# Depthwise convolution of a fused network: who builds the block matrices, who adds the taps, who sums the chunks

## The chip, the cores and the metric

One Trainium2 chip, one of its cores. The metric is the device time of one execution in microseconds, the median of several. The kernel is one program for a whole small network of four layers on 512 tokens with 1024 features.

## The reference, cut to what matters

The first block has two layers. Layer 0 is an attention mixer with an MLP behind it; layer 1 is a convolution mixer with an MLP behind it. The second block (a recurrent and a linear-attention layer) isn't touched. The convolution mixer is

```
a = h @ w_pw1 + b_pw1                                  # 1024 -> 2048
u = a[..., :1024] * sigmoid(a[..., 1024:])
u = causal_depthwise_conv(u, w_dw) + b_dw              # 31 taps, each feature by itself
u = silu(layernorm(u, ln_g, ln_b))                     # over the 1024 features
return u @ w_pw2 + b_pw2
```

The MLP is `square(relu(h @ w1)) @ w2` with 4096 hidden features. All of it is float32 in and out.

## The kernel before, in words

**Products.** A weight matrix streams in "units" of 128x1024 numbers through rings of four slots. For each unit ScalarE rounds the weights (`w_hi`, line 1247), GpSimd subtracts to get the rest (`w_lo`, line 2564), and TensorE multiplies three times (lines 670 to 672: high by high, low by high, high by low). ScalarE may round unit u+3 once TensorE has finished unit u-1, so GpSimd has the time of three units to bring in the rest of a unit before TensorE needs it. Each engine runs its own program in order; they meet at semaphores only.

**The convolution.** Features lie on the partitions, in 8 chunks of 128. For each chunk g the product `pw1{g}` (two units, 16 for the eight chunks) gives the linear part and the gate. VectorE multiplies both by the row of reciprocal norms (`by_row`, line 1841), ScalarE takes the sigmoid (line 1465), and VectorE makes the gated input `conv_u` of the chunk (lines 2113, 2116). Then the 31 taps of a chunk are done in one of three ways:

- Chunks 0, 2 and 7, and taps 0 to 25 of chunk 3, on VectorE: one multiply-and-add over 128x512 for each tap (line 2075), in two running sums that alternate ("lanes", function `tap`). Chunks 0 and 7 are split into two sums that one more add joins (line 2088).
- Chunk 1, and taps 26 to 30 of chunk 3, on two engines: ScalarE multiplies (`tap_product`, line 1448) into one of three `conv_product` buffers, and GpSimd adds (`add_product`, line 2616). Product n therefore waits for the add of product n-3. The last seven products go into the space of chunk 4's block matrices once TensorE has used them (`LATE`).
- Chunks 4, 5 and 6 on TensorE: SyncE's DMAs turn the input into four phases (`conv_phases`), and 9 matmuls a phase with block matrices (`conv_toeplitz`) give the result (line 941, 216 rows in the trace). ScalarE copies it out with the bias (line 1473) and DMAs turn it back into `conv_c` (line 2758). The block matrices of a chunk are built by four instructions (`build_toeplitz`, line 430): chunk 6's on VectorE beside layer 0's MLP (`TOEP_EARLY`), chunk 5's on VectorE right after that MLP and ahead of everything of the convolution, chunk 4's on GpSimd between the splits of the first `pw1` units (`TOEP_POOL`).

Chunk g's taps for ScalarE and GpSimd are handed out at rows k = 1, 3, 5 and 7 of the eight rows of each later `pw1` product, on ScalarE as on GpSimd; what is left is done behind `pw17`.

**The mean.** TensorE then sums the features over the partitions by a product with a matrix of ones into one bank, in this order: chunks 4, 5 (line 949), 1 (951), 6 (953), 3 (955), the sum of chunks 0 and 2 which GpSimd makes in `conv_sum` (957, the sum is line 2640), and 7 (959). Each of these seven is two matmul rows. The bank goes to VectorE, which subtracts it from every chunk (lines 2129, 2126), ScalarE squares (1481), TensorE sums the squares (967), ScalarE takes the root, VectorE the reciprocal, and normalising, silu and `pw2` follow; 34 small transposes (line 764) keep TensorE at work in between. GpSimd adds the bias of `pw2` to the residual (line 2645) as soon as it has made `conv_sum`.

Of the kernel before, what the change touches and what calls it, by code (L numbers as in the profile page):

```python
# [9 lines left out]
ALU = mybir.AluOpType  # L10
# [15 lines left out]
CONV_W = 31  # L26
# [169 lines left out]
CONV_TAPS = list(range(CONV_W))  # L196
# [3 lines left out]
PHASES = 4  # L200
# [1 line left out]
SHIFTS = (CONV_W - 1 + PHASES - 1) // PHASES + 1  # L202
PH_LEN = S // PHASES
PE_GROUPS = [(k, g) for k in PE_CHUNKS for g in range(PHASES)]
TOEP_POOL = [(4, j) for j in range(PHASES)]
TOEP_EARLY = [(6, j) for j in range(PHASES)]
TOEP_DVE = TOEP_EARLY + [(5, j) for j in range(PHASES)]
POOL_TAPS = {1: CONV_TAPS, 3: CONV_TAPS[26:]}
DVE_TAPS = {0: CONV_TAPS, 2: CONV_TAPS, 3: CONV_TAPS[:26], 7: CONV_TAPS}
POOL_ADDS = [(k, i) for k in POOL_TAPS for i in POOL_TAPS[k] if (k, i) != (1, 0)]  # L210

LATE = len(POOL_ADDS) - 7
# [15 lines left out]
def build(nc, a, out):  # L228

    ctx = ExitStack()  # L230
    with ctx:
# [62 lines left out]
        with ExitStack() as scope:  # L294
            cu = sb("conv_u", [P, KD, PAD + S], scope=scope)
            sb("place_of_conv", [P, 16], scope=scope)
            cc = sb("conv_c", [P, KD, S], scope=scope)
# [145 lines left out]
        def signal(name, keys, step=1):  # L443
            return Signal(ctx.enter_context(nc.semaphore(name)), keys, step)
# [21 lines left out]
        def done(name):  # L466
            return used.at(UNITS[name][-1])
# [57 lines left out]
        lag_in = signal("conv_lags_landed", range(PHASES * (len(PE_CHUNKS) + 2)), 16)  # L525


        part_added = signal("conv_made_on_gpsimd", TOEP_POOL + POOL_ADDS + [("sum", 2)])
        dve_tapped = signal("conv_toeplitz_then_taps_made", TOEP_DVE + [0, 2, 3, 7])
        turned_in = [signal(f"conv_turned_landed{n}",  # L530
                            [(w, k, i) for w, k in keys for i in range(PHASES)], 16)
                     for n, keys in enumerate(([("phases", k) for k in PE_CHUNKS] + [("back", 4), ("back", 6)], [("back", 5)]))]
# [127 lines left out]
        def tensor_program(e):  # L660
            w = Waits(e)
# [273 lines left out]
            for k, g in PE_GROUPS:  # L935
                b, n = PHASE_BANKS[g], PE_CHUNKS.index(k)
                empty(b)
                w.wait_ge(*phases_in(k))
                w.wait_ge(*(part_added if k == 4 else dve_tapped).at(k, PHASES - 1))
                for d in range(SHIFTS):  # L940
                    m = e.matmul(bank[b][:, 0:PH_LEN], toep[:, n, g, d, :],  # L941
                                 u4[:, n, g, d:d + PH_LEN], start=d == 0, stop=d == SHIFTS - 1)
                m.then_inc(*mean_mm.up(k, g))
                free[b] = cent_sq.at(k, g)
            empty(MEAN_BANK)
            mean = bank[MEAN_BANK]
            for k in (4, 5):
                w.wait_ge(*back_in(k))
                e.matmul(phase_of(mean[:, :]), mean_ones, phases(cc[:, k, :]), start=k == 4, stop=False)
            w.wait_ge(*part_added.at(1, CONV_W - 1))  # L950
            e.matmul(mean[:, :], mean_ones, cc[:, 1, :], start=False, stop=False)
            w.wait_ge(*back_in(6))
            e.matmul(phase_of(mean[:, :]), mean_ones, phases(cc[:, 6, :]), start=False, stop=False)
            w.wait_ge(*part_added.at(3, CONV_W - 1))
            e.matmul(mean[:, :], mean_ones, cc[:, 3, :], start=False, stop=False)
            w.wait_ge(*part_added.at("sum", 2))
            e.matmul(mean[:, :], mean_ones, csum[:, :], start=False, stop=False)
            w.wait_ge(*dve_tapped.at(7))
            e.matmul(mean[:, :], mean_ones, cc[:, 7, :], start=False, stop=True).then_inc(*mean_mm.up("mean"))

# [273 lines left out]
        def scalar_program(e):  # L1234
# [201 lines left out]
            def tap_product():  # L1436
                k, i = tap_due.pop(0)
                src, weight = cu[:, k, i:i + S], V("dw_w", k * CONV_W + i)
                w.wait_ge(*u_out.at(k))
                if (k, i) == (1, 0):  # L1440
                    e.activation(cc[:, k, :], src, ACT.Identity, scale=weight,
                                 bias=V("dw_b", k)).then_inc(*part_out.up(k, i))
                    return
                if products[0] >= LATE:
                    w.wait_ge(*mean_mm.at(PE_CHUNKS[0], PHASES - 1))
                elif products[0] >= 3:
                    w.wait_ge(part_added.sem, len(TOEP_POOL) + products[0] - 2)
                e.activation(product_at(products[0]), src, ACT.Copy, scale=weight).then_inc(*part_out.up(k, i))
                products[0] += 1

            tap_due, products = [], [0]
            for g in range(KD):
                for k in stream(f"pw1{g}"):
                    if g == 0 and k in (1, 2):
                        for kk in (2 + 2 * k, 3 + 2 * k):
                            round_x(2, kk, HIGH[kk % 4], done("up013"))
                    elif g == 0 and k == 3:
                        take_root(2)
                    elif g == 0 and k == 6:
                        copy_row(1, HIGH[2], rrow)  # L1460
                    elif g and k:
                        if k % 2 and tap_due:
                            tap_product()
                w.wait_ge(*gate_out.at(g))
                e.activation(gate[g % 2][:, :], gate[g % 2][:, :], ACT.Sigmoid,
                             bias=V("pw1_b", KD + g)).then_inc(*gated.up(g))
                tap_due += [(g, i) for i in POOL_TAPS.get(g, [])]
# [345 lines left out]
        def vector_program(e):  # L1813
# [180 lines left out]
            def mlp(layer):  # L1994
                n = 1 + 2 * layer
                for half in range(2):
                    for g in range(4):
                        if half == 0 and g == 0:
                            for k in range(4, KD):
                                split_x(n, k, other(BANKS[f"up{layer}00"])[k % 4])  # L2000
                            take_rstd(n)
                        for j in range(4):
                            w.wait_ge(*f_kept.at(layer, half, 4 * g + j))
                            if g or half:
                                w.wait_ge(*(f_lo.at(layer, half, 4 * g - 4 + j) if g else f_lo.at(layer, 0, 12 + j)))
                            e.tensor_tensor(f_square[j][:, :], f_relu[j][:, :], f_relu[j][:, :],  # L2006
                                            ALU.mult).then_inc(*f_squared.up(layer, half, 4 * g + j))
                        for j in range(4):
                            k = 4 * g + j
                            w.wait_ge(*f_hi.at(layer, half, k))  # L2010
                            e.tensor_tensor(FL[:, k, :], f_square[j][:, :], FH[:, k, :].bitcast(F32),
                                            ALU.subtract).then_inc(*f_lo.up(layer, half, k))
                        if layer == 0 and early:

                            w.wait_ge(*lag_in.last())
                            w.wait_ge(*done("dsa_out1"))
                            chunk, j = early.pop(0)
                            build_toeplitz(e, chunk, j).then_inc(*dve_tapped.up(chunk, j))
                    for m in range(2):
                        name = f"down{layer}{half}{m}"  # L2020
                        if half == 0:
                            add_tiles(BANKS[name], done(name), down_added, layer, m, n=m, scale=n)
                            continue
                        if m == 1:
                            for k in range(4):
                                split_x(n + 1, k, other(BANKS[name])[k])
                        add_tiles(BANKS[name], done(name), updated, n + 1, m, n=m, scale=n)
# [8 lines left out]
            diagonals(1, stat(2, 2))  # L2036
            w.wait_ge(*done("down011"))
            ph_padded = own_dve.after(e.memset(u4[:, :, :, 0:SHIFTS - 1], 0.0))
            for k, j in TOEP_DVE[len(TOEP_EARLY):]:
                build_toeplitz(e, k, j).then_inc(*dve_tapped.up(k, j))  # L2040

            jobs, lanes, lane_mark, turn, side_done = [], [None, None], [None, None], [0], []
# [510 lines left out]
        def gpsimd_program(e):  # L2553
# [63 lines left out]
                                ALU.add).then_inc(*part_added.up(k, i))  # L2617
                added[0] += 1

            due, added, builds = [], [0], list(TOEP_POOL)  # L2620
            for g in range(KD):
                k = 0
                for u in UNITS[f"pw1{g}"]:
                    for kk in range(units[u].per):
                        if g and k % 2 and due:
                            add_product()
                        if kk == 0:
                            split_to(u + AHEAD)
                            if builds and (g or k):
                                w.wait_ge(*lag_in.last())  # L2630
                                w.wait_ge(*done("down011"))
                                chunk, j = builds.pop(0)
                                build_toeplitz(e, chunk, j).then_inc(*part_added.up(chunk, j))
                        k += 1
                due += [(g, i) for i in POOL_TAPS.get(g, [])]
            split_to(UNITS["pw20"][0] + RING)
# [1 line left out]
                add_product()  # L2638
            w.wait_ge(*dve_tapped.at(2))
            e.tensor_tensor(csum[:, :], cc[:, 0, :], cc[:, 2, :], ALU.add).then_inc(*part_added.up("sum", 2))  # L2640

            def add_bias(n):
                w.wait_ge(*row_in.at("b_pw2"))
# [232 lines left out]
```

## Time and profile before

| | |
|---|---|
| median of 3 timed runs | 1791.7 us (1790.89, 1791.70, 1794.44) |
| the profiled execution's own time | 1793.03 us |
| its span (first to last instruction) | 1791.2 us |
| TensorE (PE) busy | 1769.1 us, 99% |
| VectorE (DVE) busy | 822.3 us, 46% |
| GpSimd (POOL) busy | 787.6 us, 44% |
| ScalarE (ACT) busy | 734.5 us, 41% |
| mean granted TensorE clock | 0.997 |

The stage of the convolution is some 140 of these 1791 us: `pw1` on TensorE from about 632 to 720.4 us, the block matrices until 744.5, the mean until 750.9, the norm until 763.3, then `pw2`. The share of an engine over the whole span says little about this stage: there VectorE and GpSimd have few pauses.

### The profile page before, as it was taken

The page shows a single profiled execution, that of the slowest core. Times are in us where ns is not written, and L with a number is a line of the kernel's source. Part 1 is how long each engine was busy: PE and PEld are TensorE (multiplying, and loading weights), DVE is VectorE, ACT ScalarE, POOL GpSimd, SP SyncE. Part 2 cuts the span into 40 slices and gives each one's busy share as a digit, 9 for nine tenths or more (in the row PEclk, how much of TensorE's full clock was granted, in tenths as well). Part 3 has the DMA queues.
Part 4 walks back from the last instruction along what each step waited for, and adds up shares of the span by engine and source line. Part 5 has one row for each costly group of instructions (what it writes and reads, how often), then busy time and mean ns, then how long its engine had stood idle before and what let it go on. Part 6 is the DMA issues. An engine that isn't in the chain of part 4 may idle for free.

```text
span 1791.2 us, 20518 instructions
## 1 busy us (share of the span) xinstructions
PE 1769.1 (99%) x8105; PEld 1452.8 (81%) x8105; DVE 822.3 (46%) x1334; ACT 734.5 (41%) x1152; POOL 787.6 (44%) x351
## 2 busy tenths in 40 slices
PE   9999999999999999999999999999999999998998
PEld 7888778888888878888888888877777888887887
DVE  4794542310121189932210121177877850358643
ACT  5534444321332334554321232355535542455543
POOL 4343224544444469834444444344544544334221
PEclk9999999999999999999999999999999999999999
DMA  6232112333332323223333332333323323232111
GB/s 208 74 108 71 59 48 81 97 106 97 103 95 94 94 82 101 77 71 95 95 94 95 102 97 95 106 107 94 95 86 91 94 94 106 71 110 72 58 60 47
DMA packets 108544, 162.51 MB, mean 91 GB/s; under 512 B 12352, under 2 KB 38592, under 8 KB 108448
## 3 DMA queue, kind: packets, MB, share of 16 engines
q1 hardware_dynamic: 108448, 161.20, 29.6%
q8 instruction: 64, 1.05, 0.2%
q14 instruction: 32, 0.26, 0.0%
HBM read 157.51 MB, written 2.10 MB: 89 GB/s over the span
## 4 chain that ended last, share of the span: by engine, by line
PE 95%; DVE 3%; ACT 1%; issue 0%; DMA 0%; DVEq 0%; SPq 0%; ACTq 0%
PE bank L670 28%; PE bank L672 28%; PE bank L671 28%; PE bank L997 1%; PE bank L941 1%; PE bank L871 1%; PE bank L756 1%; PE bank L853 1%; PE bank L1156 1%; PE bank L1141 1%; DVE rg_u L2178 1%; PE bank L861 0%; DVE rg_u L2175 0%; PE bank L1151 0%; PE bank L1122 0%
## 5 line engine op out<-in xcount | busy, mean ns | idle before, releaser
L2564 POOL TENSOR_TENSOR w_lo<-w_raw,w_hi 128x1024 fp32r<-128x1024 f32 (+1 forms) x286 | 707.1, 2477 | 956.6 <-ACT w_hi L1247 956.6
L1247 ACT ACTIVATE w_hi<-w_raw 128x1024 fp32r<-128x1024 f32 (+1 forms) x286 | 301.0, 1056 | 578.2 <-PE bank L672 572.8
L670 PE MATMUL bank<-x_hi,w_hi 128*128 128x512 f32 (+1 forms) x1264 | 503.6, 398 | 0.3 <-DVE x_lo L2354 0.3
L672 PE MATMUL bank<-x_hi,w_lo 128*128 128x512 f32 (+1 forms) x1264 | 493.0, 390 | 0.0
L671 PE MATMUL bank<-x_lo,w_hi 128*128 128x512 f32 (+1 forms) x1264 | 492.4, 390 | 0.0
L670 PEld LDWEIGHTS bank<-x_hi,w_hi 128*128 128x128 f32 (+1 forms) x1264 | 236.9, 187 | 54.3 <-issue 5.5
L671 PEld LDWEIGHTS bank<-x_lo,w_hi 128*128 128x128 f32 (+1 forms) x1264 | 237.0, 188 | 52.9 <-issue 4.8
L672 PEld LDWEIGHTS bank<-x_hi,w_lo 128*128 128x128 f32 (+1 forms) x1264 | 236.8, 187 | 50.8
L670 PE MATMUL bank<-w_hi,f_hi 128*128 128x512 f32 x512 | 200.2, 391 | 0.0
L672 PE MATMUL bank<-w_hi,f_lo 128*128 128x512 f32 x512 | 199.5, 390 | 0.0
L671 PE MATMUL bank<-w_lo,f_hi 128*128 128x512 f32 x512 | 199.4, 390 | 0.0
L2006 DVE TENSOR_TENSOR f_square<-f_relu 128x512 f32<-128x512 f32 x64 | 40.0, 687 | 260.4 <-ACT f_relu L1415 260.4
L1984 DVE SCALAR_TENSOR_TENSOR residual<-bank,norm_stats,residual 128x512 f32<-128x512 f32 x32 | 21.8, 745 | 293.8 <-PE bank L672 293.8
L670 PE MATMUL bank<-w_hi,x_hi 128*128 128x512 f32 x320 | 128.6, 402 | 6.5 <-ACT gla_v L1704 5.2
L672 PE MATMUL bank<-w_hi,x_lo 128*128 128x512 f32 x320 | 125.9, 393 | 0.0
L671 PE MATMUL bank<-w_lo,x_hi 128*128 128x512 f32 x320 | 125.8, 393 | 0.0
L672 PEld LDWEIGHTS bank<-w_hi,f_lo 128*128 128x128 f32 x512 | 96.2, 188 | 20.2
L670 PEld LDWEIGHTS bank<-w_hi,f_hi 128*128 128x128 f32 x512 | 96.2, 188 | 19.6
L671 PEld LDWEIGHTS bank<-w_lo,f_hi 128*128 128x128 f32 x512 | 96.2, 188 | 19.6
L670 PEld LDWEIGHTS bank<-w_hi,x_hi 128*128 128x128 f32 x320 | 60.7, 190 | 20.0 <-issue 7.7
L2075 DVE SCALAR_TENSOR_TENSOR bank<-conv_u,vectors,bank 128x512 f32<-128x512 f32 x109 | 74.5, 761 | 0.2
L672 PEld LDWEIGHTS bank<-w_hi,x_lo 128*128 128x128 f32 x320 | 60.6, 190 | 13.0
(332 smaller groups left out, 2093.7 us busy)
## 6 DMA issues: line engine op xcount, KB each, us to landing
w_raw<-in_mlp_w SPq DMA_DIRECT2D x128, 512.0 KB, 3.7
w_raw<-in_even_w_in SPq DMA_DIRECT2D x48, 512.0 KB, 3.8
w_raw<-in_dsa_w_in SPq DMA_DIRECT2D x28, 512.0 KB, 3.7
w_raw<-in_odd_w_in SPq DMA_DIRECT2D x24, 512.0 KB, 3.7
w_raw<-in_conv_w_pw SPq DMA_DIRECT2D x32, 256.0 KB, 3.0
w_raw<-in_even_w_out SPq DMA_DIRECT2D x16, 512.0 KB, 3.8
w_raw<-in_dsa_w_out SPq DMA_DIRECT2D x8, 512.0 KB, 3.8
w_raw<-in_conv_w_pw SPq DMA_DIRECT2D x8, 512.0 KB, 3.8
```

What stands on the lines that cost most here:

```text
L670: e.matmul(o, sh, mh, start=first, stop=False)
L671: e.matmul(o, sh, ml, start=False, stop=False)
L672: m = e.matmul(o, sl, mh, start=False, stop=last)
L756: m = e.transpose(bank[b][:, t * P:(t + 1) * P], H[:, t, k * P:(k + 1) * P], ident)
L853: e.matmul(bank[b][:, 0:n], qT[:, h, t * P:(t + 1) * P], kT[:, h, 0:n], start=True, stop=True).then_inc(*logit.up(h, t))
L871: m = e.matmul(bank[7][:, t * P:(t + 1) * P], vT[:, s, h * P:(h + 1) * P], probT[(i - 3) % 3][:, s * P:(s + 1) * P], start=s == 0, stop=s ...
L941: m = e.matmul(bank[b][:, 0:PH_LEN], toep[:, n, g, d, :], u4[:, n, g, d:d + PH_LEN], start=d == 0, stop=d == SHIFTS - 1)
L1247: e.activation(hi, src, ACT.Copy).then_inc(*w_hi.up(u))
L1984: m = e.scalar_tensor_tensor(out=hh, in0=bank[b][:, :], scalar=stat(scale, 3, t), in1=hh, op0=ALU.mult, op1=ALU.add)
L2006: e.tensor_tensor(f_square[j][:, :], f_relu[j][:, :], f_relu[j][:, :], ALU.mult).then_inc(*f_squared.up(layer, half, 4 * g + j))
L2075: m = e.scalar_tensor_tensor(out=dst, in0=src, scalar=weight, in1=total, op0=ALU.mult, op1=ALU.add)
L2564: e.tensor_tensor(lo, src, hi.bitcast(F32), ALU.subtract).then_inc(*w_lo.up(u))
```

## The change

Chunk 5's block matrices are built by VectorE beside the last down projections of layer 0's MLP; chunk 4's take their place behind the MLP, on VectorE too; GpSimd builds none. Chunk 3 is cut at tap 22 in place of 26, so four taps go from VectorE to ScalarE and GpSimd. The rows at which these two hand out a tap become k = 1, 3, 5, 6 and 7. GpSimd sums chunks 0, 2, 1 and 3 in `conv_sum` one after the other, and TensorE's mean is made of five products (4, 5, the sum, 6, 7).

```diff
-TOEP_POOL = [(4, j) for j in range(PHASES)]
+
 TOEP_EARLY = [(6, j) for j in range(PHASES)]
-TOEP_DVE = TOEP_EARLY + [(5, j) for j in range(PHASES)]
-POOL_TAPS = {1: CONV_TAPS, 3: CONV_TAPS[26:]}
-DVE_TAPS = {0: CONV_TAPS, 2: CONV_TAPS, 3: CONV_TAPS[:26], 7: CONV_TAPS}
+TOEP_DOWN = [(5, j) for j in range(PHASES)]
+TOEP_LAST = [(4, j) for j in range(PHASES)]
+POOL_TAPS = {1: CONV_TAPS, 3: CONV_TAPS[22:]}
+DVE_TAPS = {0: CONV_TAPS, 2: CONV_TAPS, 3: CONV_TAPS[:22], 7: CONV_TAPS}
...
-        part_added = signal("conv_made_on_gpsimd", TOEP_POOL + POOL_ADDS + [("sum", 2)])
-        dve_tapped = signal("conv_toeplitz_then_taps_made", TOEP_DVE + [0, 2, 3, 7])
+        part_added = signal("conv_made_on_gpsimd", POOL_ADDS + [("sum", 2), ("sum", 1), ("sum", 3)])
+        dve_tapped = signal("conv_toeplitz_then_taps_made", TOEP_EARLY + TOEP_DOWN + TOEP_LAST + [0, 3, 2, 7])
...
-                w.wait_ge(*(part_added if k == 4 else dve_tapped).at(k, PHASES - 1))
+                w.wait_ge(*dve_tapped.at(k, PHASES - 1))
...
-            w.wait_ge(*part_added.at(1, CONV_W - 1))
-            e.matmul(mean[:, :], mean_ones, cc[:, 1, :], start=False, stop=False)
+            w.wait_ge(*part_added.at("sum", 3))
+            e.matmul(mean[:, :], mean_ones, csum[:, :], start=False, stop=False)
             w.wait_ge(*back_in(6))
             e.matmul(phase_of(mean[:, :]), mean_ones, phases(cc[:, 6, :]), start=False, stop=False)
-            w.wait_ge(*part_added.at(3, CONV_W - 1))
-            e.matmul(mean[:, :], mean_ones, cc[:, 3, :], start=False, stop=False)
-            w.wait_ge(*part_added.at("sum", 2))
-            e.matmul(mean[:, :], mean_ones, csum[:, :], start=False, stop=False)
...
-                        if k % 2 and tap_due:
+                        if (k % 2 or k == 6) and tap_due:
                             tap_product()
...
+                    if layer == 0 and half == 1:
+                        w.wait_ge(*f_lo.at(0, 1, 15))
+                        for k, j in TOEP_DOWN:
+                            build_toeplitz(e, k, j).then_inc(*dve_tapped.up(k, j))
...
-            for k, j in TOEP_DVE[len(TOEP_EARLY):]:
+            for k, j in TOEP_LAST:
                 build_toeplitz(e, k, j).then_inc(*dve_tapped.up(k, j))
...
-            due, added, builds = [], [0], list(TOEP_POOL)
+            due, added = [], [0]
...
-                        if g and k % 2 and due:
+                        if g and (k % 2 or k == 6) and due:
                             add_product()
                         if kk == 0:
                             split_to(u + AHEAD)
-                            if builds and (g or k):
-                                w.wait_ge(*lag_in.last())
-                                w.wait_ge(*done("down011"))
-                                chunk, j = builds.pop(0)
-                                build_toeplitz(e, chunk, j).then_inc(*part_added.up(chunk, j))
...
             e.tensor_tensor(csum[:, :], cc[:, 0, :], cc[:, 2, :], ALU.add).then_inc(*part_added.up("sum", 2))
+            w.wait_ge(*part_added.at("sum", 2))
+            e.tensor_tensor(csum[:, :], csum[:, :], cc[:, 1, :], ALU.add).then_inc(*part_added.up("sum", 1))
+            w.wait_ge(*part_added.at("sum", 1))
+            e.tensor_tensor(csum[:, :], csum[:, :], cc[:, 3, :], ALU.add).then_inc(*part_added.up("sum", 3))
```

## Rows read from the trace of the kernel before

**Rows 1.** The chain that ended last, behind the block products: start us, us, engine, line.
```profile
720.40 24.12 PE bank L941 x216
744.52 1.72 PE bank L949 x4
...
747.11 1.12 PE bank L953 x2
748.24 0.86 PE bank L955 x2
...
750.85 0.70 DVE conv_c L2129
```
**Rows 2.** Timeline, the same stretch, the last sums: start us, us, engine, line, [idle before <-releaser].
```profile
747.50 1.27 POOL L2640 TENSOR_TENSOR conv_sum<-conv_c 128x512 f32<-128x512 f32 x1
748.70 0.69 DVE L2088 TENSOR_TENSOR conv_c<-bank,conv_c 128x512 f32<-128x512 f32 x1
748.82 0.31 PEld L957 LDWEIGHTS bank<-conv_sum,constants 128*128 128x128 f32 x2 [0.55 <-POOL conv_sum L2640]
```
**Rows 3.** Timeline of VectorE and GpSimd behind layer 0's MLP.
```profile
639.17 12.37 DVE L430 TENSOR_TENSOR conv_toeplitz<-conv_same_channel,conv_lag_weights 128x1152 f32<-128x1152 f32 x4
639.21 4.24 POOL L2564 TENSOR_TENSOR w_lo<-w_raw,w_hi 128x1024 fp32r<-128x1024 f32 x1 [2.44 <-ACT w_hi L1247]
643.41 4.07 POOL L430 TENSOR_TENSOR conv_toeplitz<-conv_same_channel,conv_lag_weights 128x1152 f32<-128x1152 f32 x1
649.34 2.20 DVE L430 TENSOR_TENSOR conv_toeplitz<-conv_same_channel,conv_lag_weights 128x1152 f32<-128x1152 f32 x1
```
**Rows 4.** Timeline of VectorE's taps: the last run of them.
```profile
730.65 15.91 DVE L2075 SCALAR_TENSOR_TENSOR bank<-conv_u,vectors,bank 128x512 f32<-128x512 f32 x24
```
**Rows 5.** Timeline of GpSimd from the split of unit 7 to the last adds.
```profile
663.74 2.41 POOL L2564 TENSOR_TENSOR w_lo<-w_raw,w_hi 128x1024 fp32r<-128x1024 f32 x1 [0.36 <-ACT w_hi L1247]
666.11 2.31 POOL L430 TENSOR_TENSOR conv_toeplitz<-conv_same_channel,conv_lag_weights 128x1152 f32<-128x1152 f32 x1
...
686.28 2.40 POOL L2564 TENSOR_TENSOR w_lo<-w_raw,w_hi 128x1024 fp32r<-128x1024 f32 x1 [1.54 <-ACT w_hi L1247]
...
715.19 2.75 POOL L2616 TENSOR_TENSOR conv_c<-conv_c,conv_product 128x512 f32<-128x512 f32 x2
718.57 2.40 POOL L2564 TENSOR_TENSOR w_lo<-w_raw,w_hi 128x1024 fp32r<-128x1024 f32 x1 [0.64 <-ACT w_hi L1247]
...
730.90 6.93 POOL L2616 TENSOR_TENSOR conv_c<-conv_c,conv_product 128x512 f32<-128x512 f32 x5
737.98 9.56 POOL L2616 TENSOR_TENSOR conv_c<-conv_c,conv_toeplitz 128x512 f32<-128x512 f32 x7
```
**Rows 6.** Timeline, gates of chunks 3 and 7: VectorE's product with the row, ScalarE's sigmoid.
```profile
683.75 0.68 DVE L1841 TENSOR_TENSOR conv_gate<-bank,rstd_row 128x512 f32<-128x512 f32 x1
721.50 0.70 DVE L1841 TENSOR_TENSOR conv_gate<-bank,rstd_row 128x512 f32<-128x512 f32 x1
722.88 0.71 ACT L1465 ACTIVATE conv_gate<-conv_gate,vectors 128x512 f32<-128x512 f32 x1
```
**Rows 7.** Timeline around layer 0's last down projections: GpSimd's splits, VectorE's pause.
```profile
545.55 4.91 POOL L2564 TENSOR_TENSOR w_lo<-w_raw,w_hi 128x1024 fp32r<-128x1024 f32 x2 [7.01 <-ACT w_hi L1247]
583.85 0.75 DVE L1984 SCALAR_TENSOR_TENSOR residual<-bank,norm_stats,residual 128x512 f32<-128x512 f32 x1 [37.98 <-PE bank L672]
```
**Rows 8.** Timeline of TensorE about 1653 us: the longest pause of the whole trace.
```profile
1648.89 0.39 PE L672 MATMUL bank<-w_hi,x_lo 128*128 128x512 f32 x1
1652.96 0.77 PE L670 MATMUL bank<-w_hi,x_hi 128*128 128x512 f32 x1 [3.69 <-ACT gla_v L1704]
```
**Rows 9.** Windows: us, PE busy, PEld, DVE, ACT, POOL, granted clock, DMA share, GB/s.
```profile
751.00:752.50 1.50, 0.15 (x1) 0.18 (x2) 1.50 (x3) 0.93 (x2) 1.50 (x3) 1.00 0.00 0
1653.00:1658.00 5.00, 5.00 (x12) 3.94 (x13) 4.90 (x4) 3.65 (x6) 4.70 (x2) 0.50 0.28 73
1659.00:1664.00 5.00, 5.00 (x24) 4.21 (x23) 4.76 (x12) 0.00 (x0) 0.00 (x0) 1.00 0.38 105
```

More of the change, by code:

```diff
@@ L1446, in tap_product @@
                 elif products[0] >= 3:
-                    w.wait_ge(part_added.sem, len(TOEP_POOL) + products[0] - 2)
+                    w.wait_ge(part_added.sem, products[0] - 2)
                 e.activation(product_at(products[0]), src, ACT.Copy, scale=weight).then_inc(*part_out.up(k, i))
```

## The prediction

> **What bounds the kernel now.** The busy shares come first: TensorE 99%, nothing else above half. So a change beside TensorE's work can only move the few places where TensorE stands, or where its work is there to wait. The chain of waits is the second view: the convolution's mean is such a place. From 744.52 us the chain runs through TensorE's seven chunk products (two rows and 0.86 us each, 1.12 for chunk 6) to VectorE's first subtraction at 750.85 [rows 1]. Third comes the timeline of that stretch, to see how near the other engines are. GpSimd ends the sum of chunks 0 and 2 at 747.50 + 1.27 = 748.77, and TensorE loads for it 0.05 us later, having idled on its load side; VectorE ends chunk 7 at 748.70 + 0.69 = 749.39 [rows 2]. All three arrive within 2 us. Here it counts which engine is loaded and which relieved.
>
> **TensorE.** Two of the seven products go: 2 x 0.86 = 1.72 us [rows 1]. If the new sum were in place when chunk 5's product ends (744.52 + 1.72 = 746.24), the subtraction would start at 749.1, 1.7 us earlier. That is the most the change can bring: the 216 block rows before it take 24.1 us whatever happens [rows 1].
>
> **VectorE.** Behind the MLP it builds four matrices as before, now chunk 4's. The four took 12.37 us, though one alone takes 2.20 [rows 3]. A split of 4.24 us and GpSimd's own build of 4.07 lie beside them, where later ones take 2.41 and 2.31 [rows 3, 5]: the two engines take turns, each instruction lengthened by about one of the other's. Without GpSimd's build one turn goes, 2.0 us, and all that follows on VectorE starts 2.0 earlier. Four taps less at 15.91 / 24 = 0.66 us [rows 4] are 2.6 more. At the last step some comes back: TensorE ends `pw17` only at 720.4 [rows 1], so the gate's product can move from 721.50 by 1.1, and the sigmoid (722.88, [rows 6]) stands on ScalarE behind a fifth tap product that waits for GpSimd; I take 2 to 3 us of standing there. Chunk 7 is then ready at about 747 to 748.5 in place of 749.39.
>
> The builds moved to layer 0 stand in a pause of 37.98 us on VectorE that ends on TensorE [rows 7]. They are 4 x 2.2 = 8.8 us, or about twice that if all take turns with splits. Nothing but the residual's add is queued behind them. The splits there (two in 4.91 us [rows 7]) get 2 us longer each, and a split has the time of three units to be ready, 16 us (in `pw1` sixteen units take the 88 us from 632 to 720.4 us, 5.5 each). Cost taken: 0; if the cover were gone, 4 x 2.0 = 8 us.
>
> The Trainium skill (GPSIMD Engine Reference, Key points) says that GpSimd shares its SBUF interfaces with VectorE and suffers beside VectorE instructions with two SBUF inputs. By that the builds, now beside layer 0's splits, would tax those splits; this case's trace agrees for the builds behind the MLP (4.24 and 4.07 us, [rows 3]) and sum and chances stay as they are if the ring has the room above.
>
> **GpSimd.** This term decides. From the split of unit 7 at 663.74 to 748.77 are 85.0 us [rows 2, 5]. In them lie 13 splits, 35 adds, one sum, one build, and 3.4 us of pauses, of which the row at 686.28 shows 1.54 and that at 718.57 shows 0.64 (two of 0.6 between them): 81.6 us of work. Added are four tap adds (39 for 35) and two sums, each dependent on the one before. A dependent add takes 1.28 with its successor 1.42 behind (five in 6.93 + the gap to 737.98 is 7.08) down to 1.37 (seven in 9.56) [rows 5]; six at 1.41 are 8.5. The build of 2.2 (663.74 to 668.29 less the split) goes. Work: 81.6 + 8.5 - 2.2 = 87.9 us. It starts 2.0 earlier, at 661.7, as the split waits for ScalarE and ScalarE for VectorE's gate. Pauses nearly vanish: a step of `pw1` holds two splits and now five adds, 2 x 2.37 + 5 x 1.35 = 11.5 us, against TensorE's 11.0 at most (two units). One stays, at chunk 3's gate (683.75 - 2.0, then sigmoid 0.7 and rounding 1.0, so 684.4 [rows 6], where GpSimd is done at 683.6), and with a bit before it I take 0.9. So the last sum ends at 661.7 + 87.9 + 0.9 = 750.5. Bounds: with a pitch of 1.28 an add (8.5 becomes 7.7) and no pause, 748.8; with 1.45 and the old 3.4 us of pauses, 753.3. I take 750.6, near to the sum, for GpSimd's time here is additive and the rows are many.
>
> Behind that sum stand chunk 6 and chunk 7 on TensorE, in order, so both wait. From the signal: 0.05, then 1.12, 0.86 and 0.87, and 0.03 to VectorE: 2.93 us. The subtraction starts at 753.5, 2.7 us later than 750.85. All behind it is a chain and moves along. The bias adds of GpSimd move by 2 us too and have until the end of `pw20`. The splits for `pw1` keep about 5 us of room before TensorE needs them, as they now have, since GpSimd starts 2 earlier and loses half a us a step.
>
> The Trainium skill (GPSIMD Engine Reference, Engine selection) has elementwise work on two inputs about twice as slow on GpSimd as on VectorE. This trace agrees: a tap is 0.66 on VectorE, 1.37 to 1.42 as an add on GpSimd alone. By the rule's factor four taps would be 5.3 us on GpSimd and 5.6 by the rows, so the last sum would come 0.3 earlier; both speak against the move.
>
> **TensorE's clock.** Between chunk 5's product (ends 746.3) and the sum (750.65) TensorE now has nothing: 4.3 us. The longest pause of the whole trace is 3.69 us, before 1652.96 [rows 8], and behind it the granted clock is 0.50, the level of 1.2 GHz, in all of 1653 to 1658: 12 rows in 5 us against 24 in 5 us once it is 1.00 again [rows 9]. Behind a pause of about 1.4 us it stayed at 1.00 [rows 9]. Before it fell TensorE had been busy until 1649.3. A pause of 4.3 is longer than the one that cost the clock. At half clock the three products take 5.2 in place of 2.6 us. Bounds: 0 (it doesn't fall, or only behind them) and 4.5 (it lasts into the squares' products, some 2 us more). One pause is one sample, so I take 2.2 as what comes of it where it falls.
>
> **Sum.** +2.7 + 2.2 = +4.9 us. Against the profiled execution's own time (1793.03, span 1791.2) that is 1797.9. The median of the timed runs is 1791.7, 1.3 lower (they spread over 3.5 us, and a fallen clock at 1653 us may be in some and not in others), so I predict 1796.6.
>
> **Rivals.**
> A, the sum is late and the clock holds: +2.7, 1794.4. For it: one pause only speaks for the fall. Against: this pause is longer.
> B, GpSimd is in time and the change is no slower than before. Place: the wait for the last sum ahead of chunks 6 and 7. It decides at 750.85 - 2.93 = 747.9: a last sum that ends sooner makes the stage shorter, down to the 1.7 us of the two products. It needs GpSimd 2.7 us faster than I count, for instance by adds that pack to 1.28, no pause, and an earlier start. With half of the two products it gives 1791.7 - 0.9 = 1790.8.
> C, GpSimd's saturation reaches further: ScalarE's products wait for adds, its copies out of the block products' banks and its roundings stand behind them, and TensorE waits for a bank or a weight. Before, the copies had over 1 us of room, and 0.3 us of a late copy I see already. With 2 us on the worse side, on top of the forecast: 1798.6.
> D, nothing of it reaches the end, since the lateness is eaten behind: 1791.7. Against: behind the mean no engine has a pause in the chain but the short ones that belong to it.
>
> **Chances.** Forecast 0.47, A 0.30, B 0.10, C 0.08, D 0.05. The range is 1791.3 to 1799.8: it takes in A, D, C and the upper bound of the clock's cost, and leaves out most of B. What this kernel's measurement can tell is 0.2%, 3.6 us. The forecast and C lie above it, the forecast with a tail below; A gives a little: slower 0.52. B reaches at most 1.7 us down, so faster is 0.03, for noise. Same 0.45.
>
> **What would show it.** Right: GpSimd without pauses from about 690 us; its last sum ending at 750 to 751; TensorE waiting some 4 us for `conv_sum` behind chunk 5's product; the subtraction at 753.5 or, with the clock down, near 756; a granted clock of 0.50 from about 750. VectorE's four builds in 10.3 us. Wrong: a last sum before 748; a pause of TensorE in `pw1` before a `w_lo`; a split in layer 0's down projections that TensorE waits for; seven rows of products still in the mean.

## The result

The changed kernel takes 1795.97 us (median of 15 runs, 1795.23 to 1798.09) against 1791.94 us of the kernel before (15 runs, 1789.82 to 1794.44): the ratio is 1.0027, 95% interval 1.0020 to 1.0034. By the medians that is 4.0 us slower, by the means of the 15 runs 4.7 (six of them lie between 1796.7 and 1798.1); forecast were 4.9 (1796.6). The profiled execution took 1795.39 us with a span of 1793.6.

The chain that ended last shows where. Its columns are start us, us, engine and line, here of the changed kernel from GpSimd's last tap add on:

```profile
745.00 1.27 POOL conv_c L2617
746.27 1.23 POOL conv_sum L2636
747.50 0.07 issue
747.57 1.27 POOL conv_sum L2638
748.84 0.07 issue
748.91 1.27 POOL conv_sum L2640
750.18 0.04 issue
750.22 2.08 PE bank L952 x2
752.30 1.32 PE bank L954 x2
753.62 0.87 PE bank L956 x2
754.49 0.02 issue
754.51 0.70 DVE conv_c L2130
```

Before, this stretch was seven chunk products of TensorE in a row [rows 1]; now it is an unbroken row of GpSimd's adds and sums, and TensorE comes in at 750.22. The first subtraction starts at 754.51 in place of 750.85. This trace runs 0.6 us ahead since its first microseconds (the last `pw1` row, the builds and the splits all lie 0.6 earlier), so like for like it is 4.3 us later. By chunk 4's product only 0.1 of that lead is left (744.27 against 744.36): TensorE loses 0.6 us inside the block products, of which more below. Note the sum's product, 2.08 us where one took 1.12 or 0.86: half rate.

The first part of the profile's page is of no help (TensorE's busy time even fell, from 1769.1 to 1766.4 us; two products less are 1.7 of it, the rest isn't taken apart here); the list of waits names the place. Columns: engine, tile, line, what it waited for: us in total, times, longest. The first row stands in the list of before too, with the same times; the second is new.

```profile
PE bank L671 <- ACT gla_v L1701: 5.2, 2, 3.7
PE bank L952 <- POOL conv_sum L2640: 4.1, 1, 4.1
```

The timeline of the changed kernel beside the moved builds, the splits next to them, and the pauses of GpSimd and VectorE in the `pw1` stretch:

```profile
544.96 10.95 POOL L2565 TENSOR_TENSOR w_lo<-w_raw,w_hi 128x1024 fp32r<-128x1024 f32 x3 [7.01 <-ACT w_hi L1244]
545.30 16.90 DVE L431 TENSOR_TENSOR conv_toeplitz<-conv_same_channel,conv_lag_weights 128x1152 f32<-128x1152 f32 x4
583.26 2.73 DVE L1981 SCALAR_TENSOR_TENSOR residual<-bank,norm_stats,residual 128x512 f32<-128x512 f32 x4 [21.05 <-PE bank L673]
...
638.59 10.42 DVE L431 TENSOR_TENSOR conv_toeplitz<-conv_same_channel,conv_lag_weights 128x1152 f32<-128x1152 f32 x4
661.21 2.41 POOL L2565 TENSOR_TENSOR w_lo<-w_raw,w_hi 128x1024 fp32r<-128x1024 f32 x1 [4.80 <-ACT w_hi L1244]
683.75 2.41 POOL L2565 TENSOR_TENSOR w_lo<-w_raw,w_hi 128x1024 fp32r<-128x1024 f32 x1 [0.51 <-ACT w_hi L1244]
719.85 0.69 DVE L1838 TENSOR_TENSOR conv_gate<-bank,rstd_row 128x512 f32<-128x512 f32 x1 [0.80 <-PE bank L673]
724.86 0.75 DVE L2117 SCALAR_TENSOR_TENSOR conv_u<-bank,vectors,conv_gate 128x512 f32<-128x512 f32 x1 [2.40 <-ACT conv_gate L1462]
```

And the windows around TensorE's pause; columns as in [rows 9], the granted clock is the third from the end:

```profile
746.00:749.00 3.00, 0.15 (x1) 0.00 (x0) 1.55 (x3) 0.00 (x0) 2.84 (x4) 1.00 0.07 22
749.00:750.00 1.00, 0.00 (x0) 0.00 (x0) 0.00 (x0) 0.00 (x0) 1.00 (x1) 0.84 0.00 0
750.00:751.00 1.00, 0.78 (x1) 0.50 (x2) 0.00 (x0) 0.00 (x0) 1.00 (x2) 0.50 0.00 0
752.00:753.00 1.00, 1.00 (x3) 0.39 (x2) 0.00 (x0) 0.00 (x0) 1.00 (x2) 0.50 0.00 0
753.00:754.00 1.00, 1.00 (x4) 0.41 (x2) 0.00 (x0) 0.00 (x0) 1.00 (x2) 0.95 0.00 0
```

TensorE was busy until 746.1, had nothing for 4.07 us, and found its clock at 0.50, the level of 1.2 GHz, until some 753.1.

### The profile page after: what moved, and what is told of

It reads as the page before. It is cut to its first block, busy times and chain, and to the rows that moved or that the text cites. A ratio compares the mean times of both kernels' runs of the same rounds, so it can differ in the third digit from the quotient of the medians.

```text
span 1793.6 us, 20521 instructions
## 1 busy us (share of the span) xinstructions
PE 1766.4 (98%) x8101; PEld 1449.1 (81%) x8101; DVE 834.9 (47%) x1334; ACT 737.5 (41%) x1156; POOL 789.1 (44%) x353
## 4 chain that ended last, share of the span: by engine, by line
PE 88%; DVE 6%; POOL 2%; issue 2%; ACT 1%; DMA 0%; SPq 0%; DVEq 0%; POOLq 0%; ACTq 0%
PE bank L671 27%; PE bank L673 26%; PE bank L672 26%; POOL conv_c L2617 2%; PE bank L994 1%; DVE bank L2076 1%; PE bank L872 1%; PE bank L854 1%; PE bank L757 1%; DVE rg_u L2179 1%; PE bank L1153 1%; PE bank L1138 1%; PE bank L862 0%; DMA residual<-in_x 0%; DVE conv_toeplitz L431 0%
```

## The experiments

Theory L: the last sum of GpSimd is late, and TensorE's pause for it costs the clock on top. Rival C: the cost lies in the builds beside layer 0's MLP. Rival H: the clock's fall costs nothing. Rival S: the moved taps and the fifth slot cost by themselves. Lines of a version differ by a few from those of the changed kernel; "before" is the kernel before in the same comparison (21 to 31 runs, medians 1791.3 to 1792.3).

The letters are those of the expectations below and not those of the prediction's rivals, which come up again at the end. "Like for like" counts from the last `pw1` row of each trace, for the traces differ by up to 0.9 us in where that row lies.

### One part alone: the builds

The kernel before with the matrices of chunks 5 and 4 built as in the change, nothing else (the lines that build and wait are left out here):

```diff
-TOEP_POOL = [(4, j) for j in range(PHASES)]
+TOEP_DOWN = [(5, j) for j in range(PHASES)]
+TOEP_LAST = [(4, j) for j in range(PHASES)]
...
```

> The kernel before with the builds moved and nothing else: chunk 5's beside layer 0's MLP, chunk 4's behind it on VectorE, none on GpSimd; four product slots a step, taps cut at 26, seven products in the mean. Theory L: VectorE and GpSimd run 2 us or more ahead, TensorE's seven products in a row still set the subtraction, so no change: 1791.9, within 0.5. Rival C: most of the 4 us is here, 1795 to 1796.

Measured: 1791.90 us against 1791.87, ratio 0.9999 (0.9991 to 1.0008). Rival C falls. The timeline also shows why a relief that is real brings nothing:

```profile
745.54 1.28 POOL L2639 TENSOR_TENSOR conv_sum<-conv_c 128x512 f32<-128x512 f32 x1
747.28 0.69 DVE L2092 TENSOR_TENSOR conv_c<-bank,conv_c 128x512 f32<-128x512 f32 x1
748.53 1.02 PE L957 MATMUL bank<-conv_sum,constants 128*128 128x512 f32 x2
749.39 1.02 PE L959 MATMUL bank<-conv_c,constants 128*128 128x512 f32 x2
750.45 2.48 DVE L2133 TENSOR_TENSOR conv_c<-conv_c,bank 128x512 f32<-128x512 f32 x4 [2.48 <-PE bank L959]
```

GpSimd and VectorE are done 2.0 and 1.4 us sooner than in [rows 2], 1.5 and 1.0 like for like, and nothing of it counts, for TensorE's seven products set the subtraction. It lies 0.4 us before that of [rows 1], as the last `pw1` row does.

### One part alone: the sums

The kernel before with three sums on GpSimd and five products in the mean (TensorE's side of the edit is left out here):

```diff
+            w.wait_ge(*part_added.at("sum", 2))
+            e.tensor_tensor(csum[:, :], csum[:, :], cc[:, 1, :], ALU.add).then_inc(*part_added.up("sum", 1))
+            w.wait_ge(*part_added.at("sum", 1))
+            e.tensor_tensor(csum[:, :], csum[:, :], cc[:, 3, :], ALU.add).then_inc(*part_added.up("sum", 3))
...
```

> The kernel before with the sums of chunks 1 and 3 on GpSimd and five products in the mean, and nothing else. Theory L: the adds end at 747.5, the three sums at 751.5, the first subtraction starts at 754.4 and with the clock's fall at about 756, 4 to 5 us later than before: 1796.5. Rival C: the mean isn't what costs, so two products less bring up to 1.7 us: 1790.2 to 1791.9.

Measured: 1797.37 us (5 runs) against 1791.87, ratio 1.0035 (1.0022 to 1.0047). The whole loss, and some 1.4 us more than that of the complete change, is in this part. The timeline:

```profile
749.36 1.26 POOL L2640 TENSOR_TENSOR conv_sum<-conv_sum,conv_c 128x512 f32<-128x512 f32 x1
750.68 2.07 PE L951 MATMUL bank<-conv_sum,constants 128*128 128x512 f32 x2 [5.28 <-POOL conv_sum L2640]
752.54 1.91 PE L953 MATMUL bank<-conv_c,constants 128*128 128x512 f32 x2
754.25 1.33 PE L955 MATMUL bank<-conv_c,constants 128*128 128x512 f32 x2
755.62 1.88 DVE L2125 TENSOR_TENSOR conv_c<-conv_c,bank 128x512 f32<-128x512 f32 x3 [7.08 <-PE bank L955]
```

### The change without its sums

```diff
-            w.wait_ge(*part_added.at("sum", 3))
+            w.wait_ge(*part_added.at(1, CONV_W - 1))
...
+            w.wait_ge(*part_added.at("sum", 2))
...
```

> The changed kernel with only the mean put back: GpSimd makes the sum of chunks 0 and 2 alone, seven products as before; builds, the tap split at 22 and the fifth slot stay. Theory L: GpSimd's adds end near 746.2 us as in the changed kernel, its one sum at 747.5, so TensorE's seven products run in a row without a pause and the time is that of the kernel before, 1791.9 within 0.5. Rival S (the fifth slot and the four taps cost by themselves, since they hold up ScalarE's sigmoid and VectorE stood 2.4 us for it): 1793 to 1794.

Measured: 1791.95 us against 1791.33, ratio 1.0004 (0.9995 to 1.0013). So the builds, the fifth slot and the four taps don't make the 4 us: rival S falls as the cause. Its list of waits has no row of TensorE waiting for a chunk or a sum in the mean. But these parts aren't free. The trace shows TensorE standing in the block products:

```profile
720.02 8.20 PE L942 MATMUL bank<-conv_phases,conv_toeplitz 128*128 128x128 f32 x72
728.46 16.34 PE L942 MATMUL bank<-conv_phases,conv_toeplitz 128*128 128x128 f32 x144 [0.24 <-ACT conv_u L1474]
```

From their first row to the mean's first (744.64) are 24.6 us, against 24.1 before (720.24 to 744.36). ScalarE copies the first bank out at 728.06, behind the gate of chunk 7 and a tap product that waited for GpSimd; before it did so at 725.05. Every trace with the fifth slot shows this, 0.5 to 0.6 us in all (the changed kernel's too), and the five without it don't; whether the slot or the added taps do it isn't separated, for every version has both or neither. The subtraction is 0.5 us later than before like for like; the timed runs, 0.6 us apart with an interval from -0.9 to 2.3, can't tell it from nothing.

### The change without its moved taps

The fifth slot goes with them; the kernel has the builds and the three sums of the change.

```diff
-POOL_TAPS = {1: CONV_TAPS, 3: CONV_TAPS[22:]}
+POOL_TAPS = {1: CONV_TAPS, 3: CONV_TAPS[26:]}
...
```

> The changed kernel with only the taps put back: chunk 3 cut at 26, four slots a step; builds moved and three sums on GpSimd stay. Theory L: GpSimd then ends its first sum at 746.8 as in the run with the builds alone, its last at 749.5, and the first subtraction starts at 752.4, 1.9 us later than there, with the pause still near 3.8 us, so the clock falls in most runs: 1795.3. If the moved taps were what made the sums late (rival S): near 1791.9.

Measured: 1796.01 us against 1791.33, ratio 1.0024 (1.0014 to 1.0033), as the change itself. Its timeline, with four taps less on GpSimd:

```profile
745.62 1.27 POOL L2636 TENSOR_TENSOR conv_sum<-conv_c 128x512 f32<-128x512 f32 x1
748.31 1.26 POOL L2640 TENSOR_TENSOR conv_sum<-conv_sum,conv_c 128x512 f32<-128x512 f32 x1
749.63 1.13 PE L952 MATMUL bank<-conv_sum,constants 128*128 128x512 f32 x2 [3.64 <-POOL conv_sum L2640]
754.13 2.48 DVE L2130 TENSOR_TENSOR conv_c<-conv_c,bank 128x512 f32<-128x512 f32 x4 [6.00 <-PE bank L956]
```

The first sum starts 0.6 us sooner than with the taps (746.22), 1.0 like for like: four more adds of 1.4 us are mostly paid by the pauses that the fifth slot fills. They aren't what made GpSimd late; the two dependent sums at the end are.

### TensorE kept at work in the pause

```diff
+            keep_warm(HIGH[0], 30)
             w.wait_ge(*part_added.at("sum", 3))
```

> The changed kernel with 30 small transposes on TensorE between chunk 5's product and the wait for the last sum, so that TensorE has work in the pause of 4.07 us. Theory L (the last sum of GpSimd is late, and the pause costs the clock on top): the last sum still ends near 750.2 us, the granted clock stays at 1.00 there, the first subtraction starts at 753.1 in place of 754.5, and the time is 1.4 us lower, 1794.6. Rival H (the fall of the clock costs nothing, since the chain waits elsewhere): 1796.0 as the changed kernel. Rival C (the cost lies in the builds moved beside layer 0's MLP): 1796.0 too.

Measured: 1794.42 us against 1791.87, ratio 1.0016 (1.0007 to 1.0025); the granted clock is 1.00 in every window from 746 to 766. The last sum is as late as before, and the products run at full rate:

```profile
746.14 3.44 PE L765 MATMUL bank<-constants 128*128 128x128 f32 x30
749.10 1.26 POOL L2641 TENSOR_TENSOR conv_sum<-conv_sum,conv_c 128x512 f32<-128x512 f32 x1
750.42 1.13 PE L953 MATMUL bank<-conv_sum,constants 128*128 128x512 f32 x2 [0.84 <-POOL conv_sum L2641]
753.30 2.48 DVE L2131 TENSOR_TENSOR conv_c<-conv_c,bank 128x512 f32<-128x512 f32 x4 [5.47 <-PE bank L957]
```

Rival H falls: against its own runs of the kernel before the loss is 2.6 us in place of 4.0, so some 1.5 us of it go with the clock's fall.

### Chunk 6 ahead of the wait: a miss

```diff
-            w.wait_ge(*part_added.at("sum", 3))
-            e.matmul(mean[:, :], mean_ones, csum[:, :], start=False, stop=False)
             w.wait_ge(*back_in(6))
             e.matmul(phase_of(mean[:, :]), mean_ones, phases(cc[:, 6, :]), start=False, stop=False)
+            w.wait_ge(*part_added.at("sum", 3))
+            e.matmul(mean[:, :], mean_ones, csum[:, :], start=False, stop=False)
```

> The changed kernel with chunk 6's product ahead of the wait for the last sum in place of behind it. Theory L: only the sum and chunk 7 are left behind the wait, so 0.9 us less, and the pause shrinks to about 2.5 us; if the clock then holds, 1.2 us more are saved: 1793.6 to 1795.1, I take 1794.0. Rival H: 1795.1. Rival C: 1796.0, for the mean would not be what costs.

Measured: 1797.15 us against 1791.87 (8 runs; two near 1794.3, six from 1796.7 to 1798.1), ratio 1.0028 (1.0018 to 1.0039). I took 1794.0, and only two runs are near it. The windows of its profile:

```profile
747.00:748.30 1.30, 1.12 (x2) 0.30 (x2) 0.69 (x1) 0.00 (x0) 1.22 (x2) 1.00 0.00 0
748.30:750.30 2.00, 0.00 (x0) 0.00 (x0) 0.00 (x0) 0.00 (x0) 1.92 (x3) 0.77 0.00 0
750.30:758.00 7.70, 6.11 (x10) 3.08 (x11) 3.82 (x6) 2.73 (x5) 7.70 (x8) 0.50 0.00 0
758.00:760.00 2.00, 2.00 (x7) 1.63 (x6) 2.00 (x3) 1.49 (x3) 2.00 (x2) 0.60 0.00 0
```

A pause cut in two held the clock no better in this profile. TensorE waited 0.9 us, did 1.12 us of chunk 6's product and waited 2.07 us, and the clock was at 0.50 from about 749.4 until past 759, into the squares' products, where the changed kernel's was back at 753.1. This is the profile of the slowest of the eight runs. What decides how long it stays low is not shown by these runs.

The same with TensorE kept at work in both parts of the pause:

```diff
+            keep_warm(HIGH[0], 8)
             w.wait_ge(*back_in(6))
             e.matmul(phase_of(mean[:, :]), mean_ones, phases(cc[:, 6, :]), start=False, stop=False)
+            keep_warm(HIGH[0], 17)
             w.wait_ge(*part_added.at("sum", 3))
```

> The changed kernel with chunk 6's product ahead of the wait for the last sum, as in the run that came out at 1797.2, and 8 small transposes ahead of it and 17 behind it on TensorE. Theory L, with what that run showed added (the clock fell at a pause of 2.07 us there and stayed low for 9.6 us, into the squares' products): with the clock held at 1.00 the reorder gives its 0.9 us, 1793.5. If the reorder were bad for another reason: 1794.4 or more, as with the transposes alone.

Measured: 1793.31 us against 1791.33, ratio 1.0011 (1.0002 to 1.0020). That is 1.1 us less than with the transposes alone by the two medians, 0.6 less if each is taken against its own kernel before. The traces show the 0.9 that was expected: like for like the subtraction comes 0.92 us sooner (752.48 against 753.30, the last `pw1` row at 719.60 and 719.50).

### The pause of the last layer, and the two terms apart

The timed runs of every kernel so far spread over 3 us, about as much as the effects. The pause of [rows 8] is a suspect: in the profile before the clock was at 0.50 for 6.8 us there (6.0 of them behind the pause), in that of the change for 3.4 us. The timed runs of the kernel before show that their spread goes with the clock, though not where it fell: in the four comparisons of this document the 40 with a mean granted clock of 0.997 took 1792.5 us on average, the 47 at 0.998 1791.3, and the two at 1.000 1789.4 and 1789.6.

```diff
+            keep_warm(HIGH[0], 30)
             for k in by_tokens("gv1", LOW, X, x5, tile_sig=tile_mm):
```

> The kernel before with 30 small transposes on TensorE ahead of gv1 of the last layer, where it stands for 3.69 us and the clock is then at 0.50 for about 6 us in the profile of before (4 us in that of the changed kernel). It isolates what a fallen clock costs in a kernel that is otherwise the same, and whether this place makes the spread of the timed runs. Theory L: the pause stays, the clock holds, and the 6 us at half rate shrink by 2 to 3 us: 1789.2, with a spread under 1.5 us. Rival H (behind the pause the chain waits for VectorE and ScalarE anyway): 1791.5 as before.

Measured: 1789.86 us (11 runs, 1789.53 to 1790.72) against 1792.25 (21 runs, 1789.35 to 1793.09), ratio 0.9989 (0.9980 to 0.9998). By the medians the kernel before gets 2.4 us shorter (0.4 to 3.6 by the interval), the granted clock is 1.00 all through this place, and the spread falls from 3.7 to 1.2 us. With this pause quiet the terms can be told apart. Of the next two versions of the changed kernel the first has the transposes in both pauses, the second only ahead of `gv1`.

> The changed kernel with the 30 transposes in both pauses: ahead of the last sum's product and ahead of gv1. Neither pause then costs the clock, so against the kernel before with the transposes ahead of gv1 (1789.9) the late sum stands alone. Theory L: 753.1 less 750.85 and 0.6 by which that trace ran earlier, 2.9 us: 1792.5, with a spread near 1.2 us. If the late sum were half hidden behind the mean: 1791.3 or less.

Measured: 1792.44 us (11 runs, ten of them 1792.12 to 1792.86). Less 1789.86 this is 2.6 us for the late sum alone, but the two ran on different chips (see below).

> The changed kernel with the 30 transposes ahead of gv1 only. Against the one with both it shows the clock's fall at the mean alone. Theory L: 1.4 us in the profile of the changed kernel, more where the fall comes earlier or lasts into the squares: 1794.0, single runs from 1792.5 (no fall) to 1796.5. Rival H: 1792.5, as with both.

Measured: 1794.60 us (11 runs, 1793.55 to 1796.27). Less 1792.44 this is 2.2 us for the clock's fall at the mean, between 1.1 and 3.8 in single runs. Its timeline, the same instructions with the clock low for longer than in the profile of the changed kernel:

```profile
748.65 1.26 POOL L2641 TENSOR_TENSOR conv_sum<-conv_sum,conv_c 128x512 f32<-128x512 f32 x1
749.97 2.08 PE L952 MATMUL bank<-conv_sum,constants 128*128 128x512 f32 x2 [4.07 <-POOL conv_sum L2641]
751.84 1.91 PE L954 MATMUL bank<-conv_c,constants 128*128 128x512 f32 x2
753.54 1.84 PE L956 MATMUL bank<-conv_c,constants 128*128 128x512 f32 x2
755.42 1.88 DVE L2131 TENSOR_TENSOR conv_c<-conv_c,bank 128x512 f32<-128x512 f32 x3 [8.01 <-PE bank L956]
```

The four kernels with transposes ahead of `gv1` ran in two comparisons, whose runs of the kernel before had medians of 1792.25 and 1791.38. The two of the clock's term ran side by side, so its 2.2 us stand. Those of the late sum did not: 2.6 us is the difference of the two medians, and against each one's kernel before it is 3.4. The traces lie between: like for like the subtraction comes 3.0 us later (753.25 and 750.67, the last `pw1` row at 719.44 and 719.82). So the late sum cost 2.6 to 3.4 us.

### A version meant to beat both

Cut at tap 23, and the sum of chunks 0, 2 and 1 made before chunk 3's adds, so that nothing is left behind the last add (TensorE's six products are left out here):

```diff
+                if (k, i) == (3, POOL_TAPS[3][0]):
+                    w.wait_ge(*dve_tapped.at(2))
+                    e.tensor_tensor(csum[:, :], cc[:, 0, :], cc[:, 2, :], ALU.add).then_inc(*part_added.up("sum", 2))
+                    w.wait_ge(*part_added.at("sum", 2))
+                    e.tensor_tensor(csum[:, :], csum[:, :], cc[:, 1, :], ALU.add).then_inc(*part_added.up("sum", 1))
...
```

> A version meant to beat both: the changed kernel with chunk 3 cut at tap 23, GpSimd's sum of chunks 0, 2 and 1 made right behind chunk 1's last add, ahead of chunk 3's adds, and chunk 3 with a product of its own (4, 5, the sum, 6, 3, 7: six products). Theory L: GpSimd ends its last add at about 747.6 us and VectorE chunk 7 at 748.3, both before TensorE comes to them, so six products in a row: 0.9 us less than seven, first subtraction at 749.8 to 750.2, 1791.2. If GpSimd or VectorE is later than that, 1791.9 to 1793.

Measured: 1791.79 us against 1791.33, ratio 1.0002 (0.9993 to 1.0011). The mean went as expected, six products in a row and no wait in it:

```profile
747.38 0.69 DVE L2091 TENSOR_TENSOR conv_c<-bank,conv_c 128x512 f32<-128x512 f32 x1
748.75 1.02 PE L958 MATMUL bank<-conv_c,constants 128*128 128x512 f32 x2
749.80 2.48 DVE L2132 TENSOR_TENSOR conv_c<-conv_c,bank 128x512 f32<-128x512 f32 x4 [1.73 <-PE bank L958]
```

But a product less, 0.9 us, didn't show in the time. The trace says why: the fifth slot and added taps are in this version too, and the block products take 24.7 us in place of 24.1, with TensorE waiting 0.32 us for ScalarE's copy of a bank. Of the 0.9 us 0.3 are left: the subtraction is 30.6 us behind the last `pw1` row, 30.8 before.

> The version with the early sum and the cut at tap 23, with the same 30 transposes ahead of gv1. The early-sum version moved the first subtraction 0.5 us ahead and came out at 1791.8 against 1791.3 of the kernel before, unresolved under a spread of 3 us. Theory L: with the spread of the clock gone its gain of 0.5 to 0.9 us shows against the kernel before with the transposes: 1788.5, and both kernels of the study are beaten. If it gains nothing: the same as the kernel before with the transposes.

Measured: 1789.71 us against 1792.25, ratio 0.9987 (0.9978 to 0.9995), 0.15 us below the kernel before with the same transposes. The early sum gains nothing that can be told from noise; its trace shows 0.3 us again. Nearly all of the gain over both kernels of the study is the transposes ahead of `gv1`.

## Why the prediction was right

- **Where.** Forecast: the change acts at the mean, by the last sum. Shown: the sums alone give the whole loss and more, and the change without them gives none that can be told in the time.
- **GpSimd.** The last sum was to end at 750.6; it ended at 750.17 in a trace that runs 0.6 ahead, so 750.8. Pauses were to vanish but for 0.9 us; the rows show 0.51 at chunk 3's gate, one of 0.25 at chunk 2's, and one of 0.43 behind the first of the last seven adds. Unit 7's split began at 661.21 (661.7 forecast).
- **VectorE.** Builds in 10.42 us (10.3 forecast); a wait of 0.80 us for `pw17` and of 2.40 us for the sigmoid (2 to 3). Chunk 7 was ready at 747.66, which was of no use.
- **The path behind the sum.** 2.93 us were counted from signal to subtraction; with the clock held it took 750.42 less 0.05 to 753.30, 2.93. In total 2.7 us were forecast for the late sum; 2.6 to 3.4 were measured, 3.0 in the traces.
- **The clock.** From one pause of 3.69 us the fall was taken as likely and 2.2 us as its price; it fell in the profile and cost 2.2 in the comparison with the transposes, but only 1.4 in the profile of the change. Here the right size is part luck: the clock stayed low for 3.4 us in that profile and for 6.8 in that of the same program with the last layer's pause filled.
- **The builds in layer 0** took turns with the splits, 16.90 us for the four and 10.95 for three splits (a fourth, of 2.81, lies beside the last build), the doubled price of the forecast, and all of it lay in VectorE's pause (21.05 us of it were left) and in the ring's room: the kernel with the builds alone is at 0.9999. The Trainium skill (GPSIMD Engine Reference, Key points) names this contention, and the trace agrees with it here as it did behind the MLP.
- **What it left out.** The block rows were to take 24.1 us "whatever happens". They took 24.7, since ScalarE's first copy of a bank stood behind chunk 7's gate and a tap product that waited for GpSimd, the same queue that the prediction counted on for VectorE's 2.4 us. It costs the changed kernel nothing, for its mean waits for GpSimd anyway; but the most that the change could bring was some 1.1 us and not 1.7.
- **Off by size.** The sum was 4.9; the medians differ by 4.0, the means by 4.7. The terms come to 4.8 or more (2.6 to 3.4, and 2.2) once the last layer's pause is quiet. The two profiles can be added up: the subtraction is 4.3 us later like for like, 0.65 of that was gained in the first microseconds, and where `gv1` begins the changed kernel is 3.6 us behind (1656.55 against 1652.96). Its span is only 2.4 longer, for there the clock was low for 3.4 us and not 6.8. So one profile compared with the other flatters the change; against the 1797.9 that the prediction gave for the profiled execution 1795.4 is 2.5 less. That the same makes the gap between 4.9 and the medians' 4.0 is likely and not shown.
- **Rivals.** B, GpSimd in time, needed an end before 747.9 and was 2.9 us off. C, TensorE starved by the saturated GpSimd, is there in small: a wait of 0.3 us for a bank, the block rows 0.6 us longer, all of it hidden in the pause for the sum. D, the lateness eaten behind the mean, is refuted by the 3.6 us that are still there at `gv1`. A, the clock holds, would give runs near 1794.5; none of the change's 15 is below 1795.2.

## What to carry to other kernels

Before giving a product of the busiest engine to another one, see which engine arrives last there: two products saved 1.7 us on TensorE at most, and the dependent adds that replaced them stood at the very end of GpSimd's queue, and two products whose inputs had been ready waited behind them. Put such a sum where its inputs are ready, not behind the last of them, and where the trace shows the clock falling behind a pause of that length, count the pause of the matrix engine twice, once as waiting and once at the clock that follows it. When a version doesn't give what its own stage shows, count the stages around it too: here the fifth slot with its taps cost 0.6 us one stage earlier and ate most of what a product less had gained. When an effect is as small as the spread of the runs, look for the pause that makes the spread and fill it first.

## What the runs showed of the hardware

- Behind a pause of 3.69 us in the last layer the granted clock was 0.50 for 3.4 us in one profile and 6.8 in another. Filling it gave 2.4 us by the medians and took the spread of the timed runs from 3.7 to 1.2 us.
- Thirty transposes of 128x128 in a pause (3.44 us) held the granted clock at 1.00, at the mean as in the last layer.
- The clock also fell where TensorE waited 0.9 us, worked 1.12 us and waited 2.07 us; it was then at 0.50 for 10 us, with TensorE at work in 6.1 of 7.7 us of it.
- VectorE's builds and GpSimd's splits alternate by whole instructions: four builds would take 8.8 us alone (4 x 2.2); with one split beside them they took 10.42, with four 16.9. In the latter each build took 4.3 to 4.4 us, and the split beside it ended 2.1 us before it did, about the time of a build alone.
